# Down products of the light last round: from four experts interleaved to one expert after another

## The reference

```
def swiglu(x, wg, wu, wd):
    return (jax.nn.silu(x @ wg) * (x @ wu)) @ wd

def expert_block(args):
    xb, e = args
    return swiglu(xb, w_gate[e], w_up[e], w_down[e])
routed = jnp.zeros_like(x).at[tok_s].add(ybuf[dest] * w_s[:, None].astype(x.dtype))
shared = swiglu(x, ws_gate, ws_up, ws_down)
x = x + g2[:, None, :] * f          # f = routed + shared
```

## Time and profile before

| | us |
|---|---|
| median of 3 runs | 1645.76 |
| lowest, highest | 1644.56, 1647.46 |
| the profiled execution, its own time | 1650.67 |
| its span, first to last instruction | 1648.9 |
| PE busy in it | 1550.8 (94%) |
| DVE, ACT busy | 729.1, 372.2 |
| DMA, mean | 352 GB/s, 580.21 MB |
| down products of the light round (L2309) | 3.64 in each layer |

### The profile page before, as it was taken

One profiled execution on the slowest core, in us unless ns is written; L12 is line 12 of the kernel. 1 busy time (PEld: TensorE's weight loads), 2 busy tenths in 40 slices (PEclk: granted clock), 3 DMA queues, 4 the chain that ended last, 5 costly groups with the idle time before them and its releaser, 6 DMA issues. The chain is left out here.

```text
span 1648.9 us, 29907 instructions
## 1 busy us (share of the span) xinstructions
PE 1550.8 (94%) x11320; PEld 1041.5 (63%) x11320; DVE 729.1 (44%) x2024; ACT 372.2 (23%) x784; POOL 96.0 (6%) x121
## 2 busy tenths in 40 slices
PE   6999989998999999999999799998999999999996
PEld 4778765776665665665565587766565556566553
DVE  3205434216365345345345335344645435533445
ACT  2002443103121111112111255331112112111122
POOL 0000100001000000000000000000000000010000
PEclk9999999999999999999999899999999999999998
DMA  9996799328899999999899783976999999998994
GB/s 366 386 371 235 288 397 383 113 92 354 339 420 420 420 420 420 419 419 418 351 384 417 231 274 131 365 291 266 419 420 421 421 419 421 418 418 342 374 420 191
DMA packets 150666, 580.21 MB, mean 352 GB/s; under 512 B 17342, under 2 KB 62562, under 8 KB 101291
## 3 DMA queue, kind: packets, MB, share of 16 engines
q1 hardware_dynamic: 134442, 535.74, 82.0%
q0 software_dynamic: 15488, 40.92, 6.4%
q10 hardware_dynamic: 640, 2.26, 0.3%
HBM read 568.22 MB, written 26.90 MB: 361 GB/s over the span
## 5 line engine op out<-in xcount | busy, mean ns | idle before, releaser
L2378 PE MATMUL ps<-ring,scratch 128*64 128x256 f32 x3840 | 428.3, 382 | 17.9 <-DMA ring<-in_moe_w_up 16.7
L2378 PEld LDWEIGHTS ps<-ring,scratch 128*64 128x64 f32 x3840 | 289.5, 138 | 143.8 <-issue 27.6
L2426 PE MATMUL ps<-ring,scratch 128*64 128x512 f32 x960 | 214.6, 597 | 0.0
L2339 PE MATMUL ps<-scratch 128*128 128x264 bf16 x1488 | 183.7, 277 | 5.1 <-issue 4.3
L2763 DVE SCALAR_TENSOR_TENSOR scratch<-scratch,ps 128x256 f32<-128x256 f32 x64 | 30.8, 481 | 349.0 <-ACT scratch L2916 342.3
L696 PE MATMUL ps<-hT,ring 128*128 128x264 f32 x768 | 183.4, 394 | 1.3 <-ACT hT L379 1.3
L2339 PEld LDWEIGHTS ps<-scratch 128*128 128x128 bf16 x1488 | 131.8, 98 | 58.6 <-issue 20.4
L696 PEld LDWEIGHTS ps<-hT,ring 128*128 128x128 f32 x768 | 148.0, 194 | 31.7 <-issue 2.8
L2426 PEld LDWEIGHTS ps<-ring,scratch 128*64 128x64 f32 x960 | 62.4, 136 | 126.0 <-issue 93.1
L2730 DVE TENSOR_TENSOR scratch<-scratch,ps 128x264 f32<-128x264 f32 x240 | 103.2, 430 | 76.9 <-PE ps L2339 76.7
L2916 ACT ACTIVATE scratch<-ps 128x256 f32<-128x256 f32 x64 | 24.6, 384 | 441.2 <-PE ps L2378 421.5
(11 more groups left out here) (401 smaller groups left out, 1381.2 us busy)
## 6 DMA issues: line engine op xcount, KB each, us to landing
ring<-in_moe_w_gate SPq DMA_DIRECT2D x128, 1024.0 KB, 18.1
ring<-in_moe_w_up SPq DMA_DIRECT2D x128, 1024.0 KB, 18.5
ring<-in_moe_w_down SPq DMA_DIRECT2D x128, 1024.0 KB, 15.9
ring<-in_ada_w SPq DMA_DIRECT2D x48, 1024.0 KB, 12.4
ring<-in_ret_w_in SPq DMA_DIRECT2D x24, 1024.0 KB, 15.7
ring<-in_state_ret SPq DMA_DIRECT2D x16, 1024.0 KB, 14.8
out_ret_sample<-ring POOLq DMA_DIRECT2D x16, 1024.0 KB, 9.2
ring<-in_gla_w_in SPq DMA_DIRECT2D x12, 1024.0 KB, 12.0
```

Of the source, the lines that this page charges most:

```text
L2339: mm = nc.tensor.matmul(k.ps[:, c % 2, 0:T], parts_of(p)[:, s, c * P:(c + 1) * P], slot_token[:, p, :], start=(p == 0 and s == 0), stop=(p ...
L2378: mm = nc.tensor.matmul(k.ps[lo:lo + CAP, 2 + p, j * DE:(j + 1) * DE], xg[:, p, c, lo:lo + CAP], slot(k, n, DE)[:, c, :], start=(c == 0), ...
L2426: mm = nc.tensor.matmul(k.ps[lo:lo + CAP, 6 + half, :], hid_t[:, p, m, lo:lo + CAP], slot(k, n, D)[:, m, half * 512:(half + 1) * 512], sta ...
```

## The change

PE no longer waits for all four down matrices before the first down product. For each expert in turn, 0 to 3, it waits for that expert's matrix and issues the expert's four matmuls, both halves, and then releases its slot. Successive matmuls of one expert write the same 32 partitions. `s_dn` is raised after half 0 of expert 3, and the slot of expert 3 is released after its half 1. The heavy round's call of `four_down` stays as it was; the parameter `of` is dropped, with its value for the heavy round as the only one.

```
+        def light_down(pe, r, e, lo):
+
+            n = place("moe_w_down", e, LIGHT_PLACE)
+            pe.wait_ge(k.ring_full[n % RING], 16 * (r + n // RING + 1))
+            for half in range(2):
+                for m in range(FC):
+                    mm = nc.tensor.matmul(k.ps[lo:lo + 32, 6 + half, :], hid_t[:, 0, m, lo:lo + 32],
+                                          slot(k, n, D)[:, m, half * 512:(half + 1) * 512],
+                                          start=(m == 0), stop=(m == FC - 1))
+                if half == 0 and e == EPI - 1:
+                    mm.then_inc(s_dn, 1)
+            mm.then_inc(k.ring_free[n % RING], 1)
+
-        def four_down(p, blocks, half, of=PLACE):
+        def four_down(p, blocks, half):
...
-                    n = place("moe_w_down", e, of)
+                    n = place("moe_w_down", e)
...
                 pe.wait_ge(s_hidtc, d + 1)
-                wait_light(pe, r, "moe_w_down")
-                for half in range(2):
-                    four_down(0, LIGHT_BLOCKS, half, LIGHT_PLACE)
+                for e, lo in LIGHT_BLOCKS:
+                    light_down(pe, r, e, lo)
```

## The result

The changed kernel is slower. In the first comparison it took 1657.4 us (median of 4 runs) against 1645.83 us (4 runs), ratio 1.0066 with a 95% interval of 1.0048 to 1.0083; in a second one, on another series of runs, 1656.84 us (6 runs) against 1645.49 us (23 runs), ratio 1.0062, 1.0048 to 1.0076. The second ratio is 10.2 us, between 7.9 and 12.5 (the medians themselves are 11.6 and 11.4 apart). I had forecast 1663.8, 18.0 us slower, with a range from 1658 to 1670.

What follows compares the result with a forecast made beforehand. PE, busy 94% of the span, was taken to bound the kernel; 9.1 us longer down products in each of two layers, less 0.2 for the wait, gave 18.0 on the 1645.76 median: 1663.8 us, range 1658 to 1670.

Steps and rivals of the forecast that it cites:

- the hand-over: Down products, between experts: the next expert's first instruction starts beside the last one, 0.05 us each, three times per layer.
- My bounds: Down products, each layer: 8.9 us longer with a step of 0.42, 10.3 longer if the hand-over doesn't overlap.
- The step of 0.43 us within an expert: Down products: one expert's instructions start 0.43 us apart, priced by columns streamed; 4 x 7 steps, 12.04 us per layer.
- The wait: Before the down products: dropping the wait for all four matrices saves 0.2 us in layer 1, nothing measurable in layer 0.
- The early start can't pay: Down products end at the later of H (hidden rows) + 12.8 and L (last landing) + 3.6: no gain.
- Nothing is absorbed: From layer 0 into GLA: no slack there in which 9 us could vanish.
- the two layers add up: Both layers' delays reach the total: 2 x 9.1 - 0.2 - 0.0 = 18.0 us.
- the chain behind keeps its distance: After the down products: casts and the chain behind them stay 0.12 and 2.13 us from the products' end.
- The clock: Behind the down products: its fall to 0.50 may shift, up to 1.5 us either way per layer; taken as 0.
- that rival: Clock goes to 0.50 within the down products: 9 us more in each layer, 1682 us; chance 7%.
- the third rival: Layer 0's delay is absorbed in GLA or the second MoE, only layer 1's 8.9 us shows: 1654.7 us; chance 6%.
- The rival of full overlap: Down products of one expert run side by side, so the order costs nothing: some 1645.3 us; chance 4%.

Runs made afterwards that it cites:

- the waits alone: Interleaved order of the kernel before, with each expert's wait ahead of its first down product, against the kernel before: 1645.97 us, ratio 1.0005.
- runs of four: Down products with half outermost, then expert, then contraction chunk, waits one by one, against the kernel before: 1645.01 us, ratio 0.9998.
- runs of six: Down products with three of each expert's four calls first, then the fourth for each, against the kernel before: 1649.75 us, ratio 1.0027.

## Why the prediction was wrong

**The step that failed** is the one at the hand-over, "At a hand-over from one expert to the next the group changes, and the next instruction can start beside the last one." The sum had 4 x 7 steps and one step saved at each of three hand-overs. The runs show four instructions beside each other there: 8 + 3 x 4 = 20 instructions in a row, 19 x 0.43 + 0.59 = 8.8, and 8.86 measured. That is 3.9 us too much for each layer, 7.9 of the 18.0. The earlier start (0.56 in both layers together, where I had 0.2) takes off 0.4 more, and the shorter gap behind the products 0.16; the 9.7 us from copy to spread are left. My bounds (8.9 and 10.3 longer) both rested on strict order and did not hold the 5.2 measured.

**The rows had it.** I wrote that "four successive instructions write four different groups". But one f32 call is two instructions, as my own description of the kernel said, and both go to one group; so before the change they went in runs of two. In strict order, 16 runs of two take 16 steps from first start to last, 7.5 us; the row had 3.64. PE had to be running ahead of a busy group already. A row of the same timeline, a little ahead of the weight loads that I had read, shows it too:

```profile
903.40 0.19 PEld L2309 LDWEIGHTS ps<-ring,scratch 128*32 128x32 f32 x8 [0.81 <-ACT scratch L2925]
```

Eight weights were loaded in the first step, two for each of the four groups. The changed kernel, whose first eight instructions all go to one group, loads two there (1625.64). The trace of before can't say how far PE runs ahead (two deep gives 3.6 as well as eight deep). Counted that way, the bounds of the new stretch are 3.6 us (eight deep) and 11.3 (two deep), and the forecast would have been a range of 0 to 15 us slower.

**The step of 0.43 us within an expert** was right: single loads stand 0.43 us apart. L831 and L1460 were the right rows for it.

**The wait** had the right direction and was too small: PE starts 0.37 us sooner in layer 1, where I had 0.2, and 0.19 in layer 0, where I had 0.0. I had taken layer 0's 0.24 as the least that a start can take, and it was not: after one wait PE starts 0.05 us behind the copy. In the second profile of the kernel before layer 0 has 0.11, so 0.13 of the 0.24 was that execution's own, and 0.06 goes with the four waits in front.

**The early start can't pay** was right in its result: the waits alone have 1.0005. The sum behind it has to be mended. By four deep, expert 3 needs its 8 steps after its own landing still, so the second term stands; the first is H + 8.9.

**Nothing is absorbed, the two layers add up, the chain behind keeps its distance** were right: 724.76 against 718.47, and 2.05 us of idle time behind the products against 2.13.

**The clock** did not fall within the down products, so that rival was wrong; the 8.9 us with one or two groups at work went at 0.43 us a step and a granted clock of 1.00. (Where the third rival names against it, the row that bears on it is the earlier trace rows, the waits of PE.) The rival of full overlap had 1645.3; the runs show that it would have held for runs of up to four. For the changed spread of layer 1 the clock gave 1.7 us back and in layer 0 0.5 (7.09 to 6.61), within the 1.5 that I had kept for each but for 0.2. In layer 0 the clock is at half for about as long as before (a mean of 0.74 over 6.61 us and of 0.76 over 7.09, 3.4 us in both) but comes over another part of the spread.

**The rule cited.** Full side-by-side work in the interleaved order was right: 3.64 us for 32 against 3.60 for 8. The estimate from the figure of the Trainium skill for packing ("TensorE: Matmul & The Clock Gate", section "Part 3: Packing small matmuls") was 15.9 us, also too much, since it too undoes all of the packing. The same section calls matmuls "strict FIFO, no reordering" in start and end. The measurements disagree: strict starts give 7.5 us for the interleaved order, where 3.64 is measured, and at least 10.9 for runs of four, where 3.70 is.

## What to carry to other kernels

When small matmuls are packed side by side in column groups (tried here in f32, with groups of 32 columns), what counts is the length of a run to one group, in instructions (two for each f32 call): up to four cost nothing, and of a longer run all but four stand alone, each for the full time of its streamed columns. So a loop may wait for its matrices one by one in runs of four (half outermost here) at no cost, but not in runs of eight. Waiting for each matrix on its own gains only if the last one's own work is shorter than all the work together; here both were 3.6 us. And before a row's count is read as so many units of program order, divide it by the instructions that one call makes.

## What the runs showed of the hardware that I had not expected

Everything measured fits one rule: PE holds up to four instructions for each group of 32 columns, one running and three waiting, and issues past a busy group until one is full. Runs of 2, 4, 6 (then 2), 8 and 16 gave 3.64, 3.70, 6.29, 8.86 and 11.50 us (the last with 256 columns), and this rule gives 3.6, 3.6, 6.2, 8.8 and 11.5. Whether it is the matmuls or their weight loads that wait there was not tried, nor was bf16 or groups of 64 columns.

The granted clock fell to half behind the down products in both layers (the kernel before), in layer 0 alone (after), in layer 1 alone (the waits alone) or in neither (runs of six, whose spreads took 5.42 and 4.62 us). It is worth 1.2 to 1.7 us each time, as much as a small edit, so an edit of that size can't be priced from one profile. Whether these edits moved the fall, or it differs between executions anyway, is not shown: the two kernels that were profiled twice had it in the same layers both times, but the mean granted clock of the timed runs of one kernel varies.
